# Hybrid decoder trunk on eight cores: attention steps reordered, roots of the norms on GpSimd, launch loads and folds rearranged

## The reference, cut to what matters

```python
h = concatenate([meta, x])                      # 2064 x 1024
for i in range(4):
    j = i // 2
    if i % 2 == 0:
        h = h + pool_mixer(rmsnorm(h, pool_norm[j]), ...)
    else:
        h = h + gla_mixer(rmsnorm(h, gla_norm[j]), ...)
return rmsnorm(h, final_norm)[16:]

# rmsnorm(x, g) = x * rsqrt(mean(x*x) + 1e-6) * g
# pool_mixer: u, z = split(h @ w_in); per group of 512 channels: trailing mean of u over 2, 4, 8
#   or 16 tokens minus u, times w_grp[g]; times scale * silu(z); @ w_out
# gla_mixer, per head and chunk, with cum = cumsum(log gate):
#   qe = q*exp(cum); ke = k*exp(-cum); att = tril(qe ke^T); o = att v + qe S
#   S = exp(cum[-1]) * (S + ke^T v)
#   y = rmsnorm_per_head(o) * head_norm * silu(z); @ w_out
```

## Time and profile before

| | |
|---|---|
| Median of 3 runs | 2133.81 us (2131.27 to 2135.88) |
| The profiled execution | 2131.31 us, its span on the slowest core 2129.8 us |
| Spans of the cores | 2122.7 to 2129.8 us, granted clock 0.984 to 0.988 |
| PE busy | 1985.5 us (93%) |
| PEld (weight loads) | 1416.1 us (66%) |
| DVE busy | 1541.8 us (72%) |
| ACT busy | 1261.1 us (59%) |
| POOL busy | 76.4 us (4%) |

### The profile page before, as it was taken

One profiled execution on the slowest core, in us unless ns is written; L12 is line 12 of the kernel. 1 busy time (PEld: TensorE's weight loads), 2 busy tenths in 40 slices (PEclk: granted clock), 3 DMA queues, 4 the chain that ended last, 5 costly groups with the idle time before them and its releaser, 6 DMA issues.

```text
span 2129.8 us, 55937 instructions; the slowest of 8 cores (2122.7 to 2129.8 us)
## 1 busy us (share of the span) xinstructions
PE 1985.5 (93%) x20056; PEld 1416.1 (66%) x20056; DVE 1541.8 (72%) x2846; ACT 1261.1 (59%) x2805; POOL 76.4 (4%) x112
## 2 busy tenths in 40 slices
PE   4789999989999999999989999998999999999997
PEld 2557677757667767766657767776667677676675
DVE  1567787867777767767767677788677677677787
ACT  3554222457777767767764332235677677676787
POOL 2110000000000000000001100000000000000000
PEclk9999999999999999999999999999999999999999
DMA  9404123140031040040012304042200400400011
GB/s 242 70 1 82 23 49 62 19 80 2 2 61 32 2 75 8 2 71 2 2 23 49 63 20 70 1 80 34 48 2 12 81 2 11 72 2 2 37 55 71
DMA packets 14977, 86.34 MB, mean 41 GB/s; under 512 B 2498, under 2 KB 2754, under 8 KB 6516
## 3 DMA queue, kind: packets, MB, share of 16 engines
q0 software_dynamic: 10720, 70.46, 19.0%
q1 hardware_dynamic: 3988, 12.30, 1.6%
HBM read 137.47 MB, written 8.39 MB: 68 GB/s over the span
## 4 chain that ended last, share of the span: by engine, by line
PE 73%; issue 9%; ACT 8%; DVE 8%; DMA 1%; DVEq 0%; ACTq 0%; POOL 0%; SPq 0%; POOLq 0%
PE ps L456 19%; PE ps L519 10%; PE ps L683 9%; PE ps L699 8%; PE ps L713 7%; PE ps L827 7%; PE ps L309 3%; PE ps L783 2%; PE ps L764 2%; DVE arena L773 2%; PE ps L760 2%; DMA h<-x 1%; ACT arena L704 1%; PE ps L383 1%; ACT hnT L329 1%
## 5 line engine op out<-in xcount | busy, mean ns | idle before, releaser
L456 PE MATMUL ps<-hnT,W 128*128 128x256 bf16 (+1 forms) x4096 | 471.0, 275 | 8.1 <-ACT arena L466 3.9
L456 PEld LDWEIGHTS ps<-hnT,W 128*128 128x128 bf16 x4096 | 402.3, 99 | 76.5 <-issue 11.9
L519 PE MATMUL ps<-W,arena 128*128 128x512 bf16 (+1 forms) x1088 | 253.1, 386 | 14.9 <-DVE arena L502 5.9
L699 PE MATMUL ps<-W,hnT 128*128 128x512 bf16 (+1 forms) x1088 | 257.1, 379 | 0.0
L683 PE MATMUL ps<-hnT,W 128*128 128x128 bf16 (+1 forms) x4288 | 256.1, 217 | 0.0
L827 PE MATMUL ps<-W,arena 128*128 128x512 bf16 (+1 forms) x1056 | 254.8, 385 | 0.0
L713 PE MATMUL ps<-hnT,W 128*128 128x128 bf16 (+1 forms) x4224 | 253.1, 217 | 0.0
L683 PEld LDWEIGHTS ps<-hnT,W 128*128 128x128 bf16 x4288 | 240.6, 98 | 2.9 <-issue 0.3
L466 ACT ACTIVATE arena<-ps 128x512 f32<-128x512 f32 (+1 forms) x128 | 77.1, 602 | 276.5 <-PE ps L456 274.5
L523 DVE TENSOR_TENSOR h<-h,ps 128x512 f32<-128x512 f32 (+1 forms) x272 | 184.3, 686 | 77.0 <-PE ps L519 66.8
L713 PEld LDWEIGHTS ps<-hnT,W 128*128 128x128 bf16 x4224 | 233.4, 98 | 0.1
(11 more groups left out here) (84 smaller groups left out, 2607.3 us busy)
## 6 DMA issues: line engine op xcount, KB each, us to landing
W<-wpack POOLq DMA_DIRECT2D x56, 1024.0 KB, 12.9
out<-h SPq DMA_DIRECT2D x16, 512.0 KB, 2.6
h<-x POOLq DMA_DIRECT2D x7, 1024.0 KB, 38.7
W<-wpack POOLq DMA_DIRECT2D x8, 512.0 KB, 12.8
h<-x SPq DMA_DIRECT2D x1, 1024.0 KB, 5.7
gbc<-pool_norm SPq DMA_DIRECT2D x2, 512.0 KB
gbc<-gla_norm SPq DMA_DIRECT2D x2, 512.0 KB
gbc<-final_norm SPq DMA_DIRECT2D x1, 512.0 KB
```

The source lines that it names most:

```text
L456: ins = e.matmul(dst[:, f, 0:n], lhsT=Wm[:, 2 * q + f, kc, :], rhs=hnT[:, kc, c0:c0 + n], start=(kc == 0), stop=(kc == 7))
L519: ins = e.matmul(po[0:nt, :], lhsT=Y[par][oc // 2][0][:, oc % 2, cc:cc + nt], rhs=Wo[:, oc, half * 512:(half + 1) * 512], start=(oc == 0), ...
L699: ins = e.matmul(pv[0:n, :], lhsT=hnT[:, kc, c0:c0 + n], rhs=Wv[:, kc, :], start=(kc == 0), stop=(kc == 7))
```

## The change

The core of the diff, cut:

```diff
@@ Prog._deps
+            if eng == "pe" and k == "pe":
+                return
@@ constants
+    nhalf = sb("nhalf", [128, NT], F32)
+    P.op("dve", lambda e: e.memset(nhalf[:], -0.5), [], [b_one])
@@ rstd_of
-            P.op("act", ... e.activation(out=lnv, in_=ssb, func=AF.Ln, scale=1.0 / D, bias=epsc) ...)
-            P.op("act", ... e.activation(out=rstd, in_=lnv, func=AF.Exp, scale=-0.5) ...)
+            P.op("pool", ... e.tensor_scalar(out=lnv, in0=ssb, scalar1=1.0 / D, scalar2=EPS, op0=ALU.mult, op1=ALU.add) ...)
+            P.op("pool", ... e.tensor_tensor(out=rstd, in0=lnv, in1=nhalf, op=ALU.pow) ...)
@@ Norm
+        def prep(self, i):
+            if not self.from_x or i >= NT:
+                return
+            stats_sq(i, "dve")
+            if i > 0:
+                stats_sq(i + 1, "act")
+            rstd_of(i, i + (2 if i > 0 else 1))
         def scale(self, i):
-            if self.from_x and (i == 0 or i % 2 == 1):
-                ...                     (stats_sq on "act" of the tile or pair, rstd_of)
-        def step(self, pbi):
+        def step(self, pbi, ahead=True):
-            self.scale(i + 1)
+            if ahead:
+                self.scale(i + 1)
@@ pool layer, block k
-                slot()
+                slot(False)
+                if g == 0:
+                    norm.prep(2 * k + 5)
...
                 G["A2"](bi, 1)
+                if g == 0:
+                    norm.scale(2 * k + 5)
@@ GLA: G is split (the scans L662 become G1), z matmuls are split in two halves
-                    P.op("pe", mz, [hnTb[ti], Wb[s][2]], PB(1))
+                    P.op("pe", lambda e: mz(e, (0, 1)), [hnTb[ti], Wb[s][2]], PB(1))
+                if midz is not None:
+                    midz()
+                if not skip(ci):
+                    P.op("pe", lambda e: mz(e, (2, 3)), [hnTb[ti], Wb[s][2]], PB(1))
@@ stageC, after the masked product L740
+                if scan is not None:
+                    scan()
@@ GLA run
                 def mid(k=k, hd=hd):
                     if hd == 0:
                         norm.gate_in(4)
-                    if k + 1 < NS:
-                        call("G", k + 1)
                     if k >= 1:
-                        call("F", k - 1)
                         call("D2", k - 1)
                 def afterqk(k=k):
-                    call("S", k - 1)
+                    if k + 1 < NS:
+                        call("G", k + 1)
+                    if k >= 1:
+                        call("S", k - 1)
                     if k >= 2:
                         maybe_final(k - 2, 1)
+                def midz(k=k):
+                    if k >= 1:
+                        call("F", k - 1)
-                call("A", k, mid=mid, afterqk=afterqk if k >= 1 else None)
-                call("C", k)
+                call("A", k, mid=mid, afterqk=afterqk, midz=midz)
+                call("C", k, scan=(lambda k=k: call("G1", k + 1)) if k + 1 < NS else None)
@@ launch
+    load_gvec(pool_norm[0:1, :])
     P.dma("sp", s_meta, ...)
     load_x(0, "sp")
-    load_gvec(pool_norm[0:1, :])
...
     load_unit(0, (0, 2, 1))
     load_x(1, "pool")
+    load_x(2, "pool")
     load_unit(0, (3,))
-    for k_ in range(2, 8):
+    norms[0].prep(0)
+    norms[0].prep(1)
+    norms[0].scale(0)
+    for k_ in range(3, 8):
         load_x(k_, "pool")
...
-    norms[0].scale(0)
     for t_ in range(3):
-        norms[0].step(6)
+        norms[0].step(6, t_ < 2)
     for dc in range(8):
-        fold(0, dc, 4 + dc % 2, "act" if dc % 2 else "dve")
+        fold(0, dc, dc, "act" if dc % 2 else "dve")
+    norms[0].prep(3)
+    norms[0].scale(3)
```

More of the change, by code:

```diff
@@ L339, in rstd_of @@
             bs_ = [b_stat[t_] for t_ in range(a_, z_)]
-            P.op("act", lambda e, r_=r_, a_=a_, z_=z_: e.activation(out=lnv[0:r_, a_:z_], in_=ssb[0:r_, a_:z_], func=AF.Ln,
-                                                                   scale=1.0 / D, bias=epsc[0:r_, 0:1]), bs_ + [b_one], bs_)
-            P.op("act", lambda e, r_=r_, a_=a_, z_=z_: e.activation(out=rstd[0:r_, a_:z_], in_=lnv[0:r_, a_:z_], func=AF.Exp,
-                                                                   scale=-0.5), bs_, bs_)
+            P.op("pool", lambda e, r_=r_, a_=a_, z_=z_: e.tensor_scalar(out=lnv[0:r_, a_:z_], in0=ssb[0:r_, a_:z_], scalar1=1.0 / D,
+                                                                       scalar2=EPS, op0=ALU.mult, op1=ALU.add), bs_, bs_)
+            P.op("pool", lambda e, r_=r_, a_=a_, z_=z_: e.tensor_tensor(out=rstd[0:r_, a_:z_], in0=lnv[0:r_, a_:z_],
+                                                                       in1=nhalf[0:r_, a_:z_], op=ALU.pow), bs_ + [b_one], bs_)
     def load_gvec(gvec_ap):
@@ L539, in run @@
                 G = groups[g]
-                slot = (lambda: norm.step(ring())) if g == 0 else (lambda: None)
+                slot = (lambda a=True: norm.step(ring(), a)) if g == 0 else (lambda a=True: None)
                 if k == 4 * NBLK - 1 and nxt is not None:
-                    slot = lambda: nxt.step(ring())
+                    slot = lambda a=True: nxt.step(ring())
                 if k == 4 * NBLK - 2 and nxt is not None:
@@ L660, in stageG, with stageG1 @@
                 P.op("act", lambda e: e.activation(out=la[:, :, 0:n], in_=la[:, :, 0:n], func=AF.Ln, bias=1.0), [b_la], [b_la])
+            def stageG1(ci):
+                c0, n, ti = chunks[ci]
                 for dc in range(2):
@@ L672, in stageG2, with stageA @@
                      [b_cum], [b_Ek])
-            def stageA(ci, mid=None, afterqk=None):
+            def stageA(ci, mid=None, afterqk=None, midz=None):
                 c0, n, ti = chunks[ci]
@@ L707, in stageA, with mz @@
                     mid()
-                def mz(e):
+                def mz(e, ecs):
                     ins = None
-                    for ec in range(4):
+                    for ec in ecs:
                         for kc in range(8):
@@ L727, in stageZ, with stageC @@
                 P.op("act", lambda e: e.activation(out=sg[:, :, 0:n], in_=sg[:, :, 0:n], func=AF.Exp, scale=-1.0), [bsg[par]], [bsg[par]])
-            def stageC(ci):
+            def stageC(ci, scan=None):
                 c0, n, ti = chunks[ci]
@@ L878, in run @@
             call("G", 0)
+            call("G1", 0)
             if before is not None:
@@ L887, in mid, with afterqk @@
                         norm.gate_in(4)
+                    if k >= 1:
+                        call("D2", k - 1)
+                def afterqk(k=k):
                     if k + 1 < NS:
@@ L890, in mid @@
                     if k >= 1:
-                        call("F", k - 1)
-                        call("D2", k - 1)
-                def afterqk(k=k):
-                    call("S", k - 1)
+                        call("S", k - 1)
                     if k >= 2:
                         maybe_final(k - 2, 1)
+                def midz(k=k):
+                    if k >= 1:
+                        call("F", k - 1)
                 if hd == 0:
@@ L941, in build @@
     load_x(1, "pool")
+    load_x(2, "pool")
     load_unit(0, (3,))
-    for k_ in range(2, 8):
+    layers = [(pool_layer if li % 2 == 0 else gla_layer)(li, 4 * li) for li in range(n_layers)]
+    norms = [Norm(li == 0, li % 2 == 1) for li in range(n_layers)]
+    norms[0].prep(0)
+    norms[0].prep(1)
+    norms[0].scale(0)
+    for k_ in range(3, 8):
         load_x(k_, "pool")
@@ L946, in build @@
         load_unit(1)
-    layers = [(pool_layer if li % 2 == 0 else gla_layer)(li, 4 * li) for li in range(n_layers)]
-    norms = [Norm(li == 0, li % 2 == 1) for li in range(n_layers)]
-    norms[0].scale(0)
     for t_ in range(3):
-        norms[0].step(6)
+        norms[0].step(6, t_ < 2)
     for dc in range(8):
-        fold(0, dc, 4 + dc % 2, "act" if dc % 2 else "dve")
+        fold(0, dc, dc, "act" if dc % 2 else "dve")
+    norms[0].prep(3)
+    norms[0].scale(3)
     pending = None
```

9 lines of the change are left out of this document (1 added, 8 removed).

## The result

The changed kernel takes 2075.5 us by the median of three runs (2075.0 to 2077.8). The ratio to the kernel before is 0.973, with a 95% interval of 0.971 to 0.975. Forecast were 2084 us, range 2061 to 2109. The profiled execution took 2077.8 us (span 2076.2 on its slowest core, granted clock 0.99). Of those that only later rows name, L466, L471, L688, L749, L760, L770, L773, L789 and L813 are now L471, L476, L700, L767, L778, L788, L791, L807 and L831.

The account below looks back on a forecast made before the run. GLA steps were taken as bound by a ring through ACT and DVE, with PE trailing; the launch and first pool layer by waits. 11.7 + 1.2 + 22.5 + 14.1 + 5.8 - 6.6 = 48.7 us gave 2084, range 2061 to 2109.

Parts of the forecast that it names:

- Launch: Up to the first block: x lands at 12.2 us, folds run without a stop, first block at 31.6 instead of 43.3; gain 11.7.
- Rival B: Launch stays bound by loads: x lands at 16.2, folds stay at 1.2 GHz, late x tiles; 2098 us, chance 0.14.
- First pool layer: Group 0, blocks 1 to 6: table switches gone, one square of each pair to DVE; 105.1 becomes 82.6 us, gain 22.5.
- The floor of 76.0 us: Blocks 1 to 6 of group 0: the second pool layer's time, taken as the least the first can reach.
- the late scale: Pool blocks: the odd tile's scale behind A2(1) stalls PE 0.8 to 1.6 us, taken as 1.1 for six blocks: 6.6.
- Second pool layer: Group 0: no x statistics to gain from, and its scale moves too; loss 6.6 us, bounds 0 and 10.
- The rebuilt ring: GLA step, L688 to next L688 through DVE and ACT in the new order: 8.82 instead of 8.90 us; GLA gain 14.1.
- Rival A: PE becomes the bound in GLA, some 8.6 us a step (9.5 in head 0): gain 48 instead of 14, 2050 us; chance 0.09.
- rival C: GLA slower: L796 heads ACT's queue waiting for S, L811, L749 and z passes stand behind it; 2145 us, chance 0.06.
- Ends of the pool layers: Roots on POOL spare ACT two table switches ahead of L466, where PE waits at both ends; gain 5.8 us.
- Rival D: Each power on GpSimd is slow: tile 1's root 4 to 6 us late, and the launch with it; 2089 us, chance 0.04.
- Self-waits: PE no longer waiting on its own matmuls: taken as 0, could bring up to 10 us, a loss excluded.

Follow-up runs that it names:

- the two runs on it: Against the changed kernel: reciprocal roots back on ScalarE in their new places, ratio 0.975; statistics issued right ahead of the scale again, root still on GpSimd, ratio 0.986.
- the run with the root ahead: Against the changed kernel, the GLA step's output-norm root (L829, L831) issued ahead of the forecast's two products (L814): 2039.6 us, ratio 0.955.

## Why the prediction was right, and where its steps were off

**The whole.** 48.7 us forecast, 53.6 measured. The sum came this near in part by luck, because the errors went opposite ways: 4 us each too much for the launch and the first pool layer, 4 too much loss in the second, 10 too little for GLA. By its own sum the forecast for the median should have been 2085 and not 2084.

**Launch, 11.7 against 7.3.** The step that failed is x's landing at 12.2 us, and with it the first scale at 13.5. I had priced the weight row ahead of x at half a tile pair, 2.9 us. Over the eight cores x lands at 15.1 us in the mean behind the row and at 8.5 ahead of it, with the weight parts on POOL's queue the same in both: 6.6 us, 0.5 of them the later issue. On the profiled core it was 17.6, past my upper bound of 16.2, and the first block came at 36.04, just past my own mark of 36. In the mean the first scale starts no earlier than before, whatever the order. Behind it the sum was better: 7.7 us to the first fold (forecast 7.1), and the folds took 8.6 us instead of 10.2. Rival B had the loads right and the slow folds wrong.

**First pool layer, 22.5 against 18.1.** The mechanism held, and by the two runs on it the place carries it, not the engine. I had told the gain as table switches gone; the run with all switches back has shorter blocks. The floor of 76.0 us was right too: without the late scale the blocks take 76.3. The late scale was a little dearer, 8.7 us instead of 6.6, since it met L471 (now L476) in five of six blocks where I had taken something between never and always. The rest, 2.0 us, is the difference between windows and ticks on the profiled core of before.

**Second pool layer, -6.6 against -2.7.** The mechanism held, the size was off: 0.6 us of wait at most instead of 1.1 in each block. There the scale starts ahead of the addition on POOL, by 0.07 us and more, and keeps its 1.28 us in all six blocks, where it takes 2.13 in five of the first layer's; that accounts for most of the difference between 1.5 and 0.6 us of wait a block. Why the two start in another order there (VectorE has no squares to make, 55.7 us busy against 66.3) is argued, not tried. What I took from the Trainium skill, GPSIMD Engine Reference, Key points, a collision in every block, would have made the loss larger; the rows show it for the first layer's scales and not for the second's.

**GLA, 14.1 against 24.1.** The rebuilt ring was right in its period (8.82 forecast, 8.77 measured, in head 0 10.01 against 9.98), and so was the sign that ACT would stand ahead of L796. As a gain the step was sized too small, 0.08 us against 0.13, and that and the heads' starts make 3.4 us in heads 0 to 2. Wrong was that final-norm steps "gain nothing": the last head of the second layer, which holds them, gave 5.7 us, and that of the first 2.3 (forecast 1.4 for the two). With the order of before 4.1 of the 5.7 go again; what in those steps became shorter is open. Rival A, TensorE as the bound, did not come about, for the reason that rival C named: with L796 ahead, L811 and all behind it stand behind its wait for S. C's place was right and its price not: it costs 37 us of what the other half of the edit brings, not more than the whole edit. Rival A's case, a ring that no longer binds, is the run with the root ahead: A had 48 us for it, and it is 37 on top of 24, 61 in all.

**Ends of the pool layers, 5.8 against 5.2; roots on GpSimd.** The ends came as reckoned. A root costs 0.9 us and not 0.3, and shows twice, 1.38 us at the launch and 2.05 in block 0, which still came out ahead of its forecast (2.1 against 1.2). Rival D did not occur. The Trainium skill, GPSIMD Engine Reference, Instruction dispatch, gives about 6 us for a first call of freshly loaded code; the first power took 0.57 us here, and the trace shows no such load.

**Self-waits, 0 against 0.** Right for this kernel, and by luck in part: the bound of 10 us looked at waits ahead of L760, while the wait that matters is one that the change itself would have made, between the halves of z.

## What to carry to other kernels

When a step is closed by a ring through several engines, an instruction that is moved ahead in a queue must be read together with its own wait: all that stands behind it in the queue inherits that wait, and a gain elsewhere can hide the loss, as 37 us were hidden here. A cost that is measured as nothing may only be covered by another bound; test it again after that bound is gone. A load moved ahead of another gains nothing if both are needed for the same instruction. And for statistics that feed the next stage, look first at when they are made and only then at the engine that makes them.

## What the runs showed of the hardware that I had not expected

- In the run with the statistics late, stops of 3 to 4 us of TensorE in each block came with a granted clock of 0.88 over the stretch, and cost nearly as much again (11.7 us) as the waits themselves had grown (13.7 us).
- A wait of TensorE on its own matmuls with four small ones in between costs 0.21 us.
- A transfer of 1 MB issued at 2 us landed between 12.8 and 17.6 us over the eight cores in one execution, and between 7.6 and 9.8 when it was issued 0.5 us earlier ahead of a broadcast row; the first scale, which needs both, moved by 0.2 us in the mean (16.4 and 16.6).
- Where VectorE's scale (two inputs of 128x1024 in float32) and GpSimd's addition (128x512) fell together, one of them was long and the other not: the scale 2.13 us and the addition 1.04 where both began at 63.91, and 1.28 and 2.10 where the scale began 0.07 us ahead.
